# Norm weights of q and k folded into one factor at the copies of transposed q, and three reorderings, in a two-layer mixer kernel

## What is computed

```python
h    = rms_norm(x) * (1 + scale1) + shift1           # scale, shift from silu(c) @ W_ada + b_ada
proj = h @ w_in                                      # then split in columns
# A: 8 heads, q and k of 96 (64 plain + 32 rotary)
q_a = rms_norm(q_a, qn_mla); k_a = rms_norm(k_a, kn_mla)   # per head: x * rsqrt(mean(x^2)) * weight
q_a, k_a = rope(last 32 of q_a), rope(last 32 of k_a)
y_a = softmax(mask(q_a k_a^T * 96**-0.5)) v_a
# B, C: 4 heads of 64 each, a linear bias with a slope per head
s   = rms_norm(q, qn) rms_norm(k, kn)^T * 64**-0.5 - slope * (qpos - kpos)
y_b = softmax(mask(s)) v_b
# C keeps, for each query, the 64 keys with the highest index score only
score = sum_h relu(iq_h . ik) * iw_h                 # 16 index heads of 32
y_c = softmax(mask(s, top_k(score, 64))) v_c
x = x + gate1 * ((sum_i sigmoid(g_i) * (y_i @ w_br_i)) @ w_out)
x = x + gate2 * swiglu(rms_norm(x) * (1 + scale2) + shift2)
```

## Time and profile before

| | us |
|---|---|
| median of 3 executions | 943.77 (943.41 to 944.41) |
| the profiled execution's own time | 944.41 |
| its span | 942.3 |
| TensorE busy / VectorE busy / ScalarE busy | 898.9 / 696.2 / 502.5 |

### The profile page before, as it was taken

One profiled execution on the slowest core, in us unless ns is written; L12 is line 12 of the kernel. 1 busy time (PEld: TensorE's weight loads), 2 busy tenths in 40 slices (PEclk: granted clock), 3 DMA queues, 4 the chain that ended last, 5 costly groups with the idle time before them and its releaser, 6 DMA issues.

```text
span 942.3 us, 12772 instructions
## 1 busy us (share of the span) xinstructions
PE 898.9 (95%) x5020; PEld 765.5 (81%) x5020; DVE 696.2 (74%) x1111; ACT 502.5 (53%) x726; POOL 27.8 (3%) x51
## 2 busy tenths in 40 slices
PE   8999989898999999999989998989899999999998
PEld 5788879776987888888868997988689778888886
DVE  5987899688797667685679967986858865575454
ACT  5554977356448443443473569844464763443441
POOL 0010000000000000000001000000000000000000
PEclk9999999999999999999999999999999999999999
DMA  9979825314643857777538973360244556555451
GB/s 376 391 289 382 318 90 179 134 46 179 268 171 142 311 209 270 280 281 281 201 132 340 364 269 134 135 223 2 90 182 179 184 180 230 208 191 187 158 179 45
DMA packets 29581, 198.12 MB, mean 210 GB/s; under 512 B 3281, under 2 KB 3793, under 8 KB 7506
## 3 DMA queue, kind: packets, MB, share of 16 engines
q1 hardware_dynamic: 23474, 155.22, 44.4%
q0 software_dynamic: 5760, 41.95, 11.6%
q10 hardware_dynamic: 288, 0.14, 0.1%
HBM read 196.24 MB, written 1.05 MB: 209 GB/s over the span
## 4 chain that ended last, share of the span: by engine, by line
PE 56%; DVE 29%; ACT 8%; issue 4%; DMA 3%; DVEq 0%; ACTq 0%
PE bank L573 13%; PE bank L575 13%; PE bank L574 13%; DVE w_lo L1352 10%; PE bank L534 3%; PE bank L535 3%; PE bank L536 3%; DMA raw<-in_slabs_dram 3%; DVE score L1544 2%; ACT w_hi L987 2%; DVE acc L1662 2%; DVE front L1359 1%; DVE score L1601 1%; PE bank L922 1%; ACT acc L1234 1%
## 5 line engine op out<-in xcount | busy, mean ns | idle before, releaser
L1352 DVE TENSOR_TENSOR w_lo<-raw,w_hi 128x2048 fp32r<-128x2048 f32 (+2 forms) x146 | 316.6, 2172 | 128.1 <-ACT w_hi L987 126.8
L987 ACT ACTIVATE w_hi<-raw 128x2048 fp32r<-128x2048 f32 (+2 forms) x146 | 264.3, 1811 | 146.8 <-PE bank L575 92.0
L573 PE MATMUL bank<-w_hi,h_hi 128*128 128x512 f32 x536 | 211.3, 394 | 8.2 <-DVE w_lo L1352 5.2
L575 PE MATMUL bank<-w_lo,h_hi 128*128 128x512 f32 x536 | 209.2, 390 | 0.0
L574 PE MATMUL bank<-w_hi,h_lo 128*128 128x512 f32 x536 | 208.9, 390 | 0.0
L573 PEld LDWEIGHTS bank<-w_hi,h_hi 128*128 128x128 f32 x536 | 100.6, 188 | 34.2 <-DVE w_lo L1352 7.7
L575 PEld LDWEIGHTS bank<-w_lo,h_hi 128*128 128x128 f32 x536 | 100.6, 188 | 21.4
L574 PEld LDWEIGHTS bank<-w_hi,h_lo 128*128 128x128 f32 x536 | 100.7, 188 | 20.3
L534 PE MATMUL bank<-h_hi,w_hi 128*128 128x256 f32 x384 | 112.3, 292 | 1.0 <-DVE w_lo L1352 1.0
L535 PE MATMUL bank<-h_lo,w_hi 128*128 128x256 f32 x384 | 109.0, 284 | 0.0
L536 PE MATMUL bank<-h_hi,w_lo 128*128 128x256 f32 x384 | 108.9, 283 | 0.0
(11 more groups left out here) (203 smaller groups left out, 1321.3 us busy)
## 6 DMA issues: line engine op xcount, KB each, us to landing
raw<-in_slabs_dram SPq DMA_DIRECT2D x124, 1024.0 KB, 4.9
front<-in_ada_dram POOLq DMA_DIRECT2D x29, 1024.0 KB, 5.6
acc<-in_ada_dram POOLq DMA_DIRECT2D x11, 1024.0 KB, 7.9
raw<-in_slabs_dram SPq DMA_DIRECT2D x16, 552.0 KB, 7.9
front<-in_ada_dram SPq DMA_DIRECT2D x5, 1024.0 KB, 11.3
raw<-in_slabs_dram SPq DMA_DIRECT2D x6, 768.0 KB, 6.9
proj<-in_ada_dram SPq DMA_DIRECT2D x2, 1024.0 KB, 9.2
x_t<-in_x_dram SPq DMA_DIRECT2D x2, 512.0 KB, 4.7
```

Source lines behind the costliest of these rows:

```text
L573: nc.tensor.matmul(o, hh, wh, start=first, stop=False)
L575: return nc.tensor.matmul(o, hh, wl, start=False, stop=final)
L987: nc.scalar.activation(w_hi[:, n % RING, 0:w], raw[:, n % RING, 0:w], ACT.Copy).then_inc(hi_ready.sem, 1)
L1352: nc.vector.tensor_tensor(w_lo[:, n % RING, 0:w], raw[:, n % RING, 0:w], w_hi[:, n % RING, 0:w], ALU.subtract).then_inc(lo_ready.sem, 1)
```

## The change

The weights of q's norm and of k's norm enter a score only as a product for each channel, so POOL multiplies the two once (`fold`), and ACT and DVE apply it when they copy turned q out of the bank. Only the rotary parts of A keep weights on DVE (products over 32 of 96 channels). The norm factor of A's q moves into the mask-and-extremum instruction, as a scale for each partition, and so does the slope of B and C; both are negated, so the maximum becomes a minimum, L1666 is dropped, and `expo` uses that minimum as its bias with scale -1. The rows of weights that are loaded shrink from 448 to 64 floats. The eight rounds of top keys of the first token tile all come ahead of the first `scores_max`, those of the second go one a step into n = 0 to 7, and C's mask moves from n = 11 to n = 8. TensorE does the scores of heads 0 and 1 between the two tiles of gate slab 7, and `gate_act(7)` comes behind the first `expo`. In the prologue the first half of `ada_sum` for k = 0 comes ahead of the reciprocal, `hi` of slab 0 ahead of the copies, TensorE has four warm-up rounds fewer (two matmuls each in the trace), the turned pieces go to banks 4 to 7, and ACT takes three banks, two of them behind k = 0's h, DVE one.

```diff
+            pool.wait_ge(vec_in.sem, 16)
+            nc.gpsimd.tensor_tensor(fold[:], cols[:, :, R_FQ:R_FQ + 3], cols[:, :, R_FK:R_FK + 3], ALU.mult)\
+                .then_inc(fold_ok.sem, 1)
...
-                    busy(3)
+                    busy(1)
...
-                    busy(6)
-
-                    pe.wait_ge(first_ca.sem, 2)
-                    pe.wait_ge(first_cv.sem, 2)
+                    busy(4)
+
+                    pe.wait_ge(first_ca.sem, 1)
+                    pe.wait_ge(first_cv.sem, 1)
                     pe.wait_ge(hi_ready.sem, hi_ready.at(l, S_A + 1))
                     pe.wait_ge(first_hi.sem, 1)
                     slot = (l * NS + S_A) % RING
                     tiles = [(bank[PA_BANKS[4 * t + cc]][:, :], slice(t * P, (t + 1) * P),
                               slice(512 * cc, 512 * (cc + 1))) for t in range(TT) for cc in range(4)]
-                    for o, at, col in tiles:
+                    for i, (o, at, col) in enumerate(tiles):
+                        if i == 6:
+
+                            pe.wait_ge(first_ca.sem, 2)
...
-                    gate_slab(l, 6 + kind)
-                pe.wait_ge(mla_out_a.sem, mla_out_a.at(l, 4))
-                pe.wait_ge(mla_out_d.sem, mla_out_d.at(l, 4))
+                    gate_slab(l, 6 + kind, (0,) if kind else (0, 1))
...
+                pe.wait_ge(mla_out_a.sem, mla_out_a.at(l, 4))
                 scores(0)
+                scores(1)
+                gate_slab(l, 7, (1,))
+                pe.wait_ge(mla_out_d.sem, mla_out_d.at(l, 4))
                 for n in range(NH + 3):
-                    if n + 1 < NH:
+                    if 1 <= n < NH - 1:
...
-                    for j in (0, 2):
-                        act.wait_ge(first_tp.sem, 4 if j else 1)
+                    hi(0, S_A)
+
+                    def turned(j):
+                        act.wait_ge(first_tp.sem, j + 1)
                         for k in (2 * j, 2 * j + 1):
-                            last = nc.scalar.activation(first_xt[k], bank[3 + j][:, (k % 2) * T:(k % 2 + 1) * T],
+                            last = nc.scalar.activation(first_xt[k], bank[FIRST_BANKS[j]][:, (k % 2) * T:(k % 2 + 1) * T],
                                                         ACT.Copy)
-                        last.then_inc(first_ca.sem, 1)
-                    hi(0, S_A)
+                        return last
+
+                    turned(0).then_inc(first_ca.sem, 1)
...
+                        if k == 0:
+                            turned(2)
+                            turned(3).then_inc(first_ca.sem, 1)
...
                     nc.scalar.activation(pq_t[:, 2 * kind:2 * kind + 2, :].rearrange("p a t -> p (a t)"),
-                                         bank[4 + 2 * kind][:, :], ACT.Copy).then_inc(pq_out.sem, 1)
+                                         bank[4 + 2 * kind][:, :], ACT.Copy, scale=fold[:, l, 2 - kind:3 - kind])\
+                        .then_inc(pq_out.sem, 1)
...
+                        by = 1.0 if kind else fold[0:A_QK, l, 0:1]
                         nc.scalar.activation(qk_t[0:A_QK, m:m + 2, :].rearrange("p a t -> p (a t)"),
-                                             bank[4 + b][0:A_QK, :], ACT.Copy).then_inc(mla_out_a.sem, 1)
+                                             bank[4 + b][0:A_QK, :], ACT.Copy, scale=by).then_inc(mla_out_a.sem, 1)
...
-                    act.wait_ge(maxed.sem, maxed.at(l, n + 1))
+                    act.wait_ge(ttr_done.sem, ttr_done.at(l, 2 * n + 2))
                     for t, (c0, c1) in enumerate(((0, P), (P, P + T))):
                         nc.scalar.activation(p_sb[n % 4][:, c0:c1], p_sb[n % 4][:, c0:c1], ACT.Exp,
-                                             bias=negmax[n % 2][:, t:t + 1], scale=slope,
+                                             bias=negmax[n % 2][:, t:t + 1], scale=-1.0,
                                              accum_out=rowsum[n % 2][:, t:t + 1]).then_inc(exped.sem, 1)
 
                 for n in range(NH + 4):
                     if n < NH:
                         expo(n)
+                    if n == 0:
+                        gate_act(l, 7)
...
+            dve.wait_ge(apro_in[0].sem, 16)
+            ada_sum(ada_pro[0], 0, A_P, (0,))
...
-                        ada_sum(ada_pro[k % 7], 0, A_P + k)
+                        ada_sum(ada_pro[k % 7], 0, A_P + k, (0, 1) if k else (1,))
                         scale_coef(0, 0, k, 1)
                         dve.sem_inc(coef_done.sem, 1)
                         if k == 0:
-                            for j in (1, 3):
-                                dve.wait_ge(first_tp.sem, 4)
-                                for kk in (2 * j, 2 * j + 1):
-                                    ins = nc.vector.tensor_copy(first_xt[kk],
-                                                                bank[3 + j][:, (kk % 2) * T:(kk % 2 + 1) * T])
-                                ins.then_inc(first_cv.sem, 1)
+                            dve.wait_ge(first_tp.sem, 2)
+                            for kk in (2, 3):
+                                ins = nc.vector.tensor_copy(first_xt[kk],
+                                                            bank[FIRST_BANKS[1]][:, (kk % 2) * T:(kk % 2 + 1) * T])
+                            ins.then_inc(first_cv.sem, 1)
...
-                    for m in range(2):
-                        gm = gains[:, g0 + HD * m:g0 + HD * (m + 1)].unsqueeze(1).unsqueeze(1)\
-                            .to_broadcast([P, TT, 4, HD])
-                        ins = nc.vector.tensor_tensor(v[:, :, 4 * m:4 * m + 4, :], v[:, :, 4 * m:4 * m + 4, :], gm,
-                                                      ALU.mult)
-                    link(ins)
...
-                link(nc.vector.tensor_tensor(qv, qv, gains[:, 0:A_QK].unsqueeze(1).to_broadcast([P, 16, A_QK]), ALU.mult))
                 rot = q4[:, :, :, A_NOPE:A_QK]
+                link(nc.vector.tensor_tensor(rot, rot, gains[:, 0:A_ROPE].unsqueeze(1).unsqueeze(1)
+                                             .to_broadcast([P, TT, A_HEADS, A_ROPE]), ALU.mult))
...
-                link(nc.vector.tensor_tensor(rot, ra, rb, ALU.add))
-
+                nc.vector.tensor_tensor(rot, ra, rb, ALU.add).then_inc(mqk_done.sem, 1)
                 dve.wait_ge(mstd_done.sem, mstd_done.at(l, 1))
                 link(nc.vector.reciprocal(ss16, ss16))
-                link(nc.vector.tensor_scalar(ss16, ss16, float(A_QK ** -0.5), None, ALU.mult))
-                nc.vector.tensor_tensor(qv, qv, ss16.unsqueeze(2).to_broadcast([P, 16, A_QK]), ALU.mult)\
-                    .then_inc(mqk_done.sem, 1)
+
+                link(nc.vector.tensor_scalar(ss16, ss16, -float(A_QK ** -0.5), None, ALU.mult))
...
-                link(nc.vector.tensor_tensor(kv[:, :, :, 0:A_NOPE], k_nope, gains[:, A_QK:A_QK + A_NOPE].unsqueeze(1)
-                                             .unsqueeze(1).to_broadcast([P, TT, A_HEADS, A_NOPE]), ALU.mult))
...
-                        nc.vector.tensor_copy(qk_t[0:A_QK, m:m + 2, :].rearrange("p a t -> p (a t)"),
-                                              bank[4 + b][0:A_QK, :]).then_inc(mla_out_d.sem, 1)
+                        dst = qk_t[0:A_QK, m:m + 2, :].rearrange("p a t -> p (a t)")
+                        if kind:
+                            ins = nc.vector.tensor_copy(dst, bank[4 + b][0:A_QK, :])
+                        else:
+                            ins = nc.vector.tensor_scalar(dst, bank[4 + b][0:A_QK, :], fold[0:A_QK, l, 0:1], None,
+                                                          ALU.mult)
+                        ins.then_inc(mla_out_d.sem, 1)
                     if kind == 0:
                         lo(l, S_GATE1 + 7)
+                top_keys(0, 8)
 
                 def scores_max(n):
                     kind, h = HEADS[n]
                     mask = {"a": causal, "b": neg_dist, "c": sel_nd[:]}[kind]
-                    slope = head_slope(kind, h)
                     dve.wait_ge(scored.sem, scored.at(l, n + 1))
                     if n >= 4:
 
                         dve.wait_ge(p_tp.sem, p_tp.at(l, n - 3))
                     for t, (c0, c1) in enumerate(((0, P), (P, P + T))):
+
+                        m = t * A_HEADS + h
+                        by = ss16[:, m:m + 1] if kind == "a" else -head_slope(kind, h)
                         nc.vector.tensor_tensor_reduce(p_sb[n % 4][:, c0:c1], bank[4 + n % 2][:, c0:c1], mask[:, c0:c1],
-                                                       1.0, NEG, ALU.add, ALU.max, rowmax[n % 2][:, t:t + 1])\
+                                                       by, -NEG, ALU.add, ALU.min, negmax[n % 2][:, t:t + 1])\
                             .then_inc(ttr_done.sem, 1)
-                    dve.wait_ge(ttr_done.sem, ttr_done.at(l, 2 * n + 2))
-                    nc.vector.tensor_scalar(negmax[n % 2], rowmax[n % 2], -slope, None, ALU.mult)\
-                        .then_inc(maxed.sem, 1)
...
```

(25 more changed lines are left out.)

39 lines of the change are left out of this document (20 added, 19 removed).

## The result

The changed kernel takes 935.88 us (935.30 to 936.97, 4 executions) against 944.09 (943.41 to 944.59) for the kernel before on the same chip: ratio 0.9914, 95% interval 0.9898 to 0.9929, 8.1 us less. Its profiled execution took 935.88 us with a span of 933.7, 8.6 less than before. The forecast was 936.1. The sum came out; its terms, and what it left unasked, are the matter of the rest.

What follows compares the result with a forecast made beforehand. TensorE, busy 898.9 of 942.3 us, was taken as the bound, so only its waits could shrink. Gains 2.35 + 0.2 + 4.7 + 3.8 - 0.4 - 3.0 = 7.65 us gave a median of 936.1, range 932.7 to 939.8.

Steps and rivals of the forecast that it cites:

- The prologue: Kernel start: TensorE's first real matmul at 15.95 us, second slab at 22.35 instead of 24.72; 2.35 us gained and kept.
- the smaller load: Weights rows ahead of slabs in SP's queue, 0.2 MB fewer: between 0 and 0.45 us once, taken as 0.2.
- a low clock here: Prologue: transposes may not count as PE-busy, so fewer warm-up rounds leave a low clock; sum loses 0.5 us at most.
- Start of the heads: Gate slabs to third scores: wait at k's transposes goes, 3.1 us wait behind top keys comes; 2.35 us a layer, 4.7 gained.
- The small waits: TensorE's short waits within the heads shrink or go: 1.8 us a layer, 3.8 with 0.2 at layer 0's `ada_sum`.
- 0.2 + 0.45 + 0.77: Heads, per layer: ACT's earlier copies at n = 7, L1666's latency at n = 7 and 8, no top-key round at n = 12.
- The wait at the end of the heads: At n = 15, a wait of 1.21 us on an ACT chain hanging on TensorE's own transpose; it stays.
- The extremum with a column: A's heads: reading the factor from a column costs 0.05 us, twice a head, on the path in a few; 0.4 lost.
- The rival that the minimum runs at a lower rate: Extremum in the heads: minimum with a factor slower than the maximum; at double time costs 10 us, 946.2; chance 0.04.
- The clock: Behind the new wait before the third scores, TensorE's clock falls again: 1.5 us lost a layer, 3.0 in all, bounds 0 to 3.4.

Runs made afterwards that it cites:

- the runs without a fall of the clock: Changed kernel with unused matmuls in TensorE's wait (931.19 us), or with three (926.36) or five (924.22) of eight top-key rounds moved ahead of DVE's lo.
- the run with filler: Changed kernel plus fourteen TensorE matmuls with unused results inside the 3.6 us wait before the third scores of each layer: 931.19 us, ratio 0.9874.

## Why the prediction was right, and where its steps were not

**The prologue** (2.35, and 0.2 for the smaller load). The first half of `ada_sum` ran in DVE's idle time and the reciprocal didn't slip, 10.49 us where I had 10.8, as the load landed at 9.28 and not 9.5. DVE, then TensorE:

```profile
9.28 1.28 DVE L1379 CUSTOM_DVE_ANT_0 front<-front,cond,cols 128x1024 f32<-128x1024 f32 x1 [1.37 <-DMA front<-in_ada_dram]
...
10.49 0.16 DVE L1480 RECIPROCAL small<-small 128x2 f32<-128x2 f32 x1
...
13.81 2.28 DVE L1372 TENSOR_TENSOR w_lo<-raw,w_hi 128x2048 fp32r<-128x2048 f32 x1
```

```profile
5.96 5.49 PE L532 MATMUL bank<-kz_t 128*128 128x256 f32 x12
...
13.81 1.89 PE L532 MATMUL bank<-kz_t 128*128 128x256 f32 x8
15.46 2.08 PE L653 MATMUL bank<-w_hi,h_hi 128*128 128x512 f32 x8
...
21.95 0.47 PE L581 MATMUL bank<-w_hi,h_hi 128*128 128x512 f32 x1 [0.77 <-DVE h_lo L1498]
```

TensorE started at 15.46, forecast 15.95, and its second slab at 21.95, forecast 22.35: 2.77 us for 2.35. Of the smaller load nothing is seen apart from this. The stage with the transposes and the first products has a granted clock of 1.00:

```profile
12.00:16.00 4.00, 4.00 (x27) 3.63 (x28) 3.66 (x6) 3.88 (x8) 0.00 (x0) 1.00 1.01 428
```

The Trainium skill, TensorE: Matmul & The Clock Gate, "Part 4: PE-mode transpose", says of a transpose that "it doesn't count as PE-busy the same way". With a low clock here the prediction had the second slab near 24.7; the trace has it at 21.95. That doesn't say how transposes are counted, only that the warm-up was enough, and by little: the twelve matmuls ahead of the transposes start 0.43 us apart, at 1.2 GHz, and the second transpose starts 0.19 us behind the first, close to the 0.21 of transposes at 1.2 GHz, before the rest follow 0.11 apart. Before, the spacing of the warm-up matmuls had gone from 0.43 to 0.22 us at 9.7 us.

**Start of the heads** (4.7). Every step held: no wait at k's transposes, copies of q 1.3 us early (1.6 forecast), TensorE idle before the third scores, for 3.60 us (3.1 forecast). The forecast's times leave out the lead of 2.26 us that the kernel has here; with it the third scores were forecast at 179.1 - 2.26 = 176.84 and came at 176.89, and TensorE ran out of work 0.45 us before its 176.0 - 2.26. Between the gate slabs and the third scores the changed kernel wins 4.57 - 2.26 = 2.3 us in layer 0 and 7.83 - 5.60 = 2.2 in layer 1, 4.5 in all.

**The small waits** (3.8). From the sixth to the last scores 1.42 and 1.43 us were won, which is the forecast's 0.2 + 0.45 + 0.77 = 1.42 to the hundredth, and 0.2 more at layer 0's `ada_sum`. Between the third and sixth scores the runs without a fall of the clock win 0.95 a layer where I had 0.4. Together 4.95: this term was 1.1 too small. The trace shows why. I had counted the waits of 0.25 and 0.19 us by the idle time in the profile, which begins at the modelled end of a matmul. From start to start, the two steps of transposed weights with these waits took 0.74 us each before, and 0.33 and 0.42 in the run with filler; with the scores between them (0.85 and 0.66) that is 0.92 a layer. The wait at the end of the heads was said to stay at 1.21 and is 1.23.

**The extremum with a column** (-0.4). By form:

```profile
L1683 DVE CUSTOM_DVE_ANT_0 acc<-bank,konst,small 128x256 f32<-128x256 f32 x16 | 7.7, 480 | 0.0
...
L1683 DVE CUSTOM_DVE_ANT_0 acc<-bank,konst,small 128x128 f32<-128x128 f32 x16 | 5.6, 349 | 3.0 <-issue 2.7
...
L1683 DVE CUSTOM_DVE_ANT_0 acc<-bank,konst 128x256 f32<-128x256 f32 x8 | 3.4, 419 | 0.0
...
L1683 DVE CUSTOM_DVE_ANT_0 acc<-bank,konst 128x128 f32<-128x128 f32 x8 | 2.3, 292 | 3.1 <-PE bank L809 2.9
```

A pair costs 0.83 - 0.71 = 0.12 us more with the column, 0.10 forecast. Since the small waits from the sixth to the last scores came to their forecast without it, nothing of it shows on the path; no run took the column away to measure it. The rival that the minimum runs at a lower rate is ruled out: without a column it takes what the maximum took.

**The clock** (-3.0). It fell where I said, but the cost was mis-sized: 2.7 and 1.3 us, 4.0 in all by the run with filler against the 3.0 forecast, since in layer 0 the stretch at 1.2 GHz was 6.7 us long and not 3.4. I had taken the length from a row of before for a constant. Where the second 3.4 us came from stays open.

**What the sum left out.** Entries that nearly cancel. Behind layer 0's wait for the index scores the slow stretch is longer in the changed profile (mean clock 0.72 over 118 to 130 us, 0.86 before), 0.9 us lost, of which 0.3 is won again before the heads; in layer 1 the one of before at 586 us is absent, and 1.9 are won up to the heads. Such stretches in the middle of a layer come and go among the profiles of these runs without any change there; they are no part of the change. A new wait of 0.51 us ahead of the gate slab at 550.37 is part of 0.75 lost between the layers, whose cause I didn't trace; 0.3 more goes between the last slabs and the end.

In all the named terms came to 2.8 + 4.5 + 4.95 - 4.0 = 8.3 us, where the forecast had 2.55 + 4.7 + 3.8 - 0.4 - 3.0 = 7.65; the rest above adds 0.25, and the span became 8.6 shorter. The forecast is near partly by luck: two misses of about 1 us (small waits too small, clock too small) have different signs, and so do the smaller ones.

**The step not taken.** The prediction asked what the change does as a whole, and never what each part does given the others. All it needed was in its own text: "Now come eight rounds of top keys ... 5.7 us ... and only then the extremum". Before, the first extremum came ahead of the rounds behind an idle time of DVE of 6.36 us. It said that TensorE would wait 3.1 us for those rounds, and priced the order with the fold as one gain. Priced against the fold in the old order, its own numbers turn the sign: in the trace of before the first scores wait 0.78 us for ACT's `gate_act`, so the order's wait of 3.1 is 2.3 more, the clock adds 1.5, and of the gains in the heads 0.4 and 0.77 (fewer rounds a step, none at n = 12) are the order's. 2.3 + 1.5 - 1.2 = 2.6 us lost a layer, 5.2 in all by this estimate, where 6.9 were measured.

## What to carry to other kernels

When one part of a change frees an engine, price the other parts against the freed schedule, not the old one: an order that hides work behind a wait is worth something as long as the wait is there (5.0 us here), and can cost when it is gone (6.3 to 6.9). Work that fills another engine's idle time belongs ahead of the instruction that is waiting there, in pieces no longer than the idle time (here 3.89 us, five rounds of 0.72), and not in one block behind it. A wait of TensorE has two prices, its length and the clock behind it; ask for the second one wherever the same trace shows a fall behind a wait of that size, and give it a range, not one number.

## What the hardware showed that I had not expected

The cost of TensorE's clock behind a wait isn't one number: at waits of equal length, 3.60 us in both layers of the changed kernel, 6.7 and 3.4 us ran at 1.2 GHz, at a price of 2.7 and 1.3 us. It isn't the layer either. With the old prologue the same two waits of 3.60 us stand in both layers, and the lengths are the other way round, 3.4 us in layer 0 and 6.7 in layer 1:

```profile
180.00:187.00 7.00, 7.00 (x42) 6.30 (x41) 5.80 (x28) 3.93 (x15) 0.00 (x0) 0.76 0.00 0
634.00:641.00 7.00, 5.67 (x24) 5.52 (x25) 6.12 (x30) 3.44 (x13) 0.00 (x0) 0.52 0.00 0
```

From the third to the sixth scores this run loses 0.54 and 1.64 us against before, where 0.95 is won without a fall: a price of 1.5 and 2.6 us.

Ahead of the heads the clock fell at waits of 2.95 to 2.97 and 3.60 us and not at 2.40, 1.52 and 0.78; waits between 2.40 and 2.95 were not tried there. But the length of the wait alone doesn't decide it. In the middle of layer 1 TensorE waits 1.42 us behind the same work in both kernels; before (first two rows) the clock fell there, in the changed kernel (last two) it did not:

```profile
585.97 0.47 PE L603 MATMUL bank<-w_hi,y_hi 128*128 128x512 f32 x1 [1.42 <-ACT front L1180]
586.00:590.00 4.00, 4.00 (x11) 3.17 (x12) 3.79 (x9) 4.00 (x9) 0.00 (x0) 0.57 0.48 203
...
582.30 0.48 PE L611 MATMUL bank<-w_hi,y_hi 128*128 128x512 f32 x1 [1.42 <-ACT front L1199]
582.00:586.00 4.00, 3.70 (x16) 3.06 (x17) 3.83 (x8) 4.00 (x9) 0.00 (x0) 1.00 0.53 223
```

So one profiled execution without a fall at some wait, as here at 1.52 us, doesn't show that such a wait is free; what decides stays open.

Fourteen matmuls of no use, 3.2 us of TensorE's time, in each layer's wait gave 3.8 to 4.7 us back.
